# Whole 8 KB rows for the gate-up matrix of the experts, with gate and up summed at the same time in two banks

## What is computed

```python
def moe_ffn(x, w_router, b_router, w_gu, b_gu, w_down, b_down):
    ...
    def expert_block(args):
        xb, e = args
        h = xb @ w_gu[e] + b_gu[e]              # w_gu[e] is 1024 x 2048
        h_gate, h_up = jnp.split(h, 2, axis=-1)
        h_gate = jnp.minimum(h_gate, SWIGLU_LIMIT)
        h_up = jnp.clip(h_up, -SWIGLU_LIMIT, SWIGLU_LIMIT)
        act = h_gate * jax.nn.sigmoid(SWIGLU_ALPHA * h_gate) * (h_up + 1.0)
        return act @ w_down[e] + b_down[e]      # w_down[e] is 1024 x 1024
```

## Time and profile before

| | us |
|---|---|
| median of 3 runs | 2260.23 |
| lowest and highest of them | 2252.01, 2263.8 |
| the profiled execution | 2261.8 |
| its span in the profile | 2260.0 |
| TensorE busy in it | 2079.9 |

### The profile page before, as it was taken

One profiled execution on the slowest core, in us unless ns is written; L12 is line 12 of the kernel. 1 busy time (PEld: TensorE's weight loads), 2 busy tenths in 40 slices (PEclk: granted clock), 3 DMA queues, 4 the chain that ended last, 5 costly groups with the idle time before them and its releaser, 6 DMA issues.

```text
span 2260.0 us, 27915 instructions
## 1 busy us (share of the span) xinstructions
PE 2079.9 (92%) x11973; PEld 1381.1 (61%) x11973; DVE 831.3 (37%) x961; ACT 698.4 (31%) x922; POOL 35.0 (2%) x26
## 2 busy tenths in 40 slices
PE   7999989999999997899998999988988988898886
PEld 6998778899899775799977544423333333333222
DVE  5555745555555584555543511111111101111102
ACT  5444454544544534444334211111111111111111
POOL 5000000000000000000000000000000000000000
PEclk9999999999999995999999999999999999999998
DMA  8555416555455440355544799999999999999995
GB/s 277 193 186 184 142 29 205 186 186 182 153 188 185 164 148 22 112 187 186 186 158 144 257 405 412 412 413 413 413 413 413 413 413 412 413 414 413 413 413 236
DMA packets 225239, 604.25 MB, mean 267 GB/s; under 512 B 12276, under 2 KB 105408, under 8 KB 208660
## 3 DMA queue, kind: packets, MB, share of 16 engines
q1 hardware_dynamic: 225140, 602.83, 71.7%
HBM read 601.70 MB, written 1.09 MB: 267 GB/s over the span
## 4 chain that ended last, share of the span: by engine, by line
PE 62%; DMA 28%; DVE 5%; ACT 2%; issue 1%; SPq 1%; ACTq 0%; DVEq 0%
PE ps L1366 14%; PE ps L1367 14%; PE ps L1368 14%; DMA sb_w_free<-in_moe_w_gate_up 12%; PE ps L1684 12%; DMA sb_raw<-in_moe_w_gate_up 7%; DMA sb_late_raw<-in_moe_w_gate_up 6%; PE ps L1667 2%; PE ps L1539 1%; PE ps L1500 1%; DMA sb_more_raw<-in_moe_w_gate_up 1%; DMA sb_raw<-in_moe_w_down 1%; PE ps L1524 1%; PE ps L1509 1%; PE ps L1386 1%
## 5 line engine op out<-in xcount | busy, mean ns | idle before, releaser
L843 DVE TENSOR_TENSOR sb_w_lo<-sb_raw,sb_w_hi 128x2048 fp32r<-128x2048 f32 x180 | 416.2, 2316 | 358.8 <-ACT sb_w_hi L582 358.4
L582 ACT ACTIVATE sb_w_hi<-sb_raw 128x2048 fp32r<-128x2048 f32 x180 | 343.9, 1914 | 295.1 <-PE ps L1368 282.8
L1366 PE MATMUL ps<-sb_xT_hi,sb_w_hi 128*128 128x256 f32 x1408 | 397.3, 282 | 7.4 <-DVE sb_xT_lo L864 7.4
L1367 PE MATMUL ps<-sb_xT_lo,sb_w_hi 128*128 128x256 f32 x1408 | 396.2, 281 | 0.0
L1368 PE MATMUL ps<-sb_xT_hi,sb_w_lo 128*128 128x256 f32 x1408 | 396.1, 281 | 0.0
L1366 PEld LDWEIGHTS ps<-sb_xT_hi,sb_w_hi 128*128 128x128 f32 x1408 | 265.9, 189 | 9.9 <-issue 4.5
L1367 PEld LDWEIGHTS ps<-sb_xT_lo,sb_w_hi 128*128 128x128 f32 x1408 | 266.0, 189 | 1.6
L1368 PEld LDWEIGHTS ps<-sb_xT_hi,sb_w_lo 128*128 128x128 f32 x1408 | 266.0, 189 | 0.0
L1684 PE MATMUL ps<-sb_raw,sb_xs 128*64 128x512 f32 x792 | 190.8, 605 | 22.8 <-DMA sb_raw<-in_moe_w_gate_up 22.8
L1684 PE MATMUL ps<-sb_w_free,sb_xs 128*64 128x512 f32 x736 | 176.8, 604 | 21.0 <-DMA sb_w_free<-in_moe_w_gate_up 20.9
L770 ACT ACTIVATE sb_x<-ps 128x512 f32<-128x512 f32 x64 | 38.2, 597 | 492.2 <-PE ps L1684 492.2
(11 more groups left out here) (236 smaller groups left out, 2340.4 us busy)
## 6 DMA issues: line engine op xcount, KB each, us to landing
sb_raw<-in_moe_w_gate_up SPq DMA_DIRECT2D x99, 1024.0 KB, 20.8
sb_w_free<-in_moe_w_gate_up SPq DMA_DIRECT2D x92, 1024.0 KB, 20.9
sb_w_free<-in_moe_w_down SPq DMA_DIRECT2D x52, 1024.0 KB, 19.4
sb_raw<-in_moe_w_down SPq DMA_DIRECT2D x45, 1024.0 KB, 18.3
sb_raw<-in_ffn_w_gate SPq DMA_DIRECT2D x44, 1024.0 KB, 5.3
sb_raw<-in_ffn_w_up SPq DMA_DIRECT2D x44, 1024.0 KB, 5.3
sb_raw<-in_ffn_w_down SPq DMA_DIRECT2D x44, 1024.0 KB, 4.9
sb_late_raw<-in_moe_w_gate_up SPq DMA_DIRECT2D x32, 1024.0 KB, 19.1
```

What stands on the lines that cost most here:

```text
L582: sc.activation(w_hi[:, c % CUT, :], raw[:, c % RAW, :], ACT.Copy).then_inc(hi_made, 1)
L843: ve.tensor_tensor(w_lo[:, c % CUT, :], raw[:, c % RAW, :], w_hi[:, c % CUT, :].bitcast(F32), ALU.subtract).then_inc(lo_made, 1)
L1366: pe.matmul(o, l_hi, r_hi, start=start, stop=False)
L1367: pe.matmul(o, l_hi, r_lo, start=False, stop=False)
```

## The change

Three things change together.

- **Loads.** The gate-up matrix of an expert is loaded in 8 chunks of 128 whole rows, 8 KB a row, one row in each partition. The down chunks stay. The order in step s is 3 gate-up chunks of the next expert, 4 down chunks of this one, 5 gate-up chunks of the next, again 12 chunks a step and 384 in all, in the same ring.
- **Sums.** A gate-up chunk feeds both sums at once, two matmuls into bank 0 (gate) and two into bank 1 (up), all four with the same 64 tokens' 128 rows as weights. Bank 2 takes down, bank 3 the picks, gathered rows and gate turned.
- **Reading.** After the last gate-up chunk ScalarE copies bank 0 and VectorE copies bank 1 to the two halves of h_rows (now 1024 wide), and TensorE turns both, gate into bank 3 and up into bank 2, at the start of the next step. The scatter now stands behind the last gate-up chunk, where it stood ahead of the last up chunk.

```diff
@@ expert_chunk, step_loads (SyncE)
-                w = a["moe_w_down_2"][0] if part == "down" else a["moe_w_gate_up_2"][0]
-                col = D if part == "up" else 0
-                rows = "e (p k) n -> p (e k) n" if part == "down" else "e (k p) n -> p (e k) n"
-                src = w[bass.ds(e, 1), 256 * j:256 * (j + 1), col:col + D].rearrange(rows, p=P)
+                if part == "down":
+                    src = a["moe_w_down_2"][0][bass.ds(e, 1), 256 * j:256 * (j + 1), :].rearrange("e (p k) n -> p (e k) n", p=P)
+                else:
+                    src = a["moe_w_gate_up_2"][0][bass.ds(e, 1), P * j:P * (j + 1), :].rearrange("e p n -> p e n")
...
+                for j in range(first, 3):
+                    expert_chunk("gate_up", e + 1, j, step_t(s) + j, laps)
                 for j in range(4):
...
+                    if 3 + j >= first:
+                        expert_chunk("down", e, j, step_t(s) + 3 + j, laps)
+                for j in range(3, 8):
+                    if 4 + j >= first:
+                        expert_chunk("gate_up", e + 1, j, step_t(s) + 4 + j, laps)
@@ ScalarE and VectorE
+            def read_gate(t, laps):
+
                 sc.wait_ge(chunk_used, used_no(t, laps))
...
+                sc.activation(h_rows[:, 0, :], ps[:, 0, :], ACT.Copy).then_inc(gate_read, 1)
...
+            def read_up(t, laps):
+
+                ve.wait_ge(chunk_used, used_no(t, laps))
+                ve.tensor_copy(h_rows[:, 1, :], ps[:, 1, :]).then_inc(up_read, 1)
@@ TensorE
+            def gate_up_rows(left, t, i, laps):
+
+                pe.wait_ge(slot_loaded[t % RING], loaded_no(t, laps))
+                for bank in range(2):
+                    for h in range(2):
+                        w = slots[t % RING][:, bank * D + h * 512:bank * D + (h + 1) * 512]
+                        ins = pe.matmul(ps[halves[h], bank, :], left(i), w, start=False, stop=i == KT - 1)
+                ins.then_inc(chunk_used, 1)
...
             def first_step(r):
...
                 bias(0, 0, 0)
+                bias(1, D, 0)
                 for j in range(4):
                     pe.wait_ge(xs_made, n + j + 1)
-                    rows(left, j, j, 0, laps)
+                    gate_up_rows(left, 2 * j, 2 * j, laps)
                     if j < 2:
                         gather(2 + j, 0, 2 + j)
...
+                    gate_up_rows(left, 2 * j + 1, 2 * j + 1, laps)
+                    if j < 2 and isinstance(r, int):
+                        residual(1, j)
...
             def step(base, base4, s, laps):
...
+                pe.wait_ge(gate_read, e + 1)
+                turn_rows(0, 3)
+                pe.wait_ge(up_read, e + 1)
+                turn_rows(1, 2)
...
+                bias(0, 0, s + 1)
+                bias(1, D, s + 1)
+                for i in range(3):
+                    gate_up_rows(left, t + i, i, laps)
+                pe.wait_ge(m_g_made, e + 1)
+                turn_picks(base4, s)
                 pe.wait_ge(m_act_made, e + 1)
...
+                for j in range(4):
+                    down_rows(t + 3 + j, j, laps)
...
+                for i in range(3, 8):
+                    gate_up_rows(left, t + 4 + i, i, laps)
                 pe.wait_ge(y_lo_made, e + 1)
                 scatter()
-                rows(left, t + 11, 3, q, laps)
```

More of the change, by code:

```diff
@@ L463, in _ @@
[L463 to L470, removed]
+                dst = slots[t % RING].rearrange("p (a n) -> p a n", a=2 if part == "down" else 1)
+                sp.dma_start(dst, src).then_inc(slot_loaded[t % RING], 16)
@@ L503, in more_loads @@
                 laps = round_laps(r)
[L504 to L507, removed]
+                for j in range(8):
+                    expert_chunk("gate_up", 0, j, j, laps)
                 with sp.Fori(0, N_E // 4 - 1) as it:
@@ L1683, in rows, with turn_rows @@
                         w = slots[t % RING][:, k * D + h * 512:k * D + (h + 1) * 512]
-                        ins = pe.matmul(ps[halves[h], bank, :], left(2 * j + k), w,
-                                        start=not biased and j == 0 and k == 0, stop=j == 3 and k == 1)
+                        ins = pe.matmul(ps[halves[h], 2, :], own(2 * j + k), w, start=j == 0 and k == 0, stop=j == 3 and k == 1)
                 ins.then_inc(chunk_used, 1)
-            def turn_rows(n, bank):
-                pe.wait_ge(h_read, n)
-                by_row = h_rows.rearrange("q (j p k) -> q j k p", j=2, k=2)
+            def turn_rows(part, bank):
+                by_row = h_rows[:, part, :].rearrange("q (j p k) -> q j k p", j=2, k=2)
                 for i in range(4):
@@ L1701, in turn_picks @@
                     for half in halves:
-                        pe.matmul(ps[half, bank, b * P:(b + 1) * P], own, ident[:], start=True, stop=True)
+                        pe.matmul(ps[half, 3, b * P:(b + 1) * P], own, ident[:], start=True, stop=True)
                 for half in halves:
@@ L1705, in turn_picks @@
                         own = pick[:, (s // 4) % 2, b, SLOTS * (s % 4):SLOTS * (s % 4 + 1)].bitcast(F32)
[L1706 removed]
+                        ins = pe.matmul(ps[half, 3, S:S + 1], own, quad_gate[:, (s // 4) % 2, b, s % 4:s % 4 + 1],
                                         start=b == 0, stop=b == 1)
@@ L1760, in step @@
-                for j in range(1, 4):
-                    rows(own, t + 4 + j, j, p, laps)
-                pe.wait_ge(m_g_made, e + 2)
-                if s < PIECES:
-                    pe.wait_ge(xs_made, e + 6)
-                bias(q, D, s + 1)
-                for j in range(3):
-                    rows(left, t + 8 + j, j, q, laps)
+                    pe.wait_ge(pickT_made, e + 1)
+                    gather(3, (s + 5) // 4, (s + 5) % 4)
+                for i in range(3, 8):
+                    gate_up_rows(left, t + 4 + i, i, laps)
@@ L1788, in last_step @@
                     ins.then_inc(down_bias_added, 1)
+                pe.wait_ge(m_g_made, e + 1)
+                turn_picks(QUADS * r, s)
                 pe.wait_ge(m_act_made, e + 1)
-                pe.wait_ge(pickT_made, e + 1)
                 for j in range(4):
-                    rows(own, t + j, j, 0, laps, biased=False)
+                    down_rows(t + j, j, laps)
                 pe.wait_ge(y_lo_made, e + 1)
```

163 lines of the change are left out of this document (67 added, 96 removed).

## The result

The changed kernel takes 2246.53 us (median of 20 runs, 2240.66 to 2263.64), the kernel before 2261.11 (20 runs, 2252.01 to 2275.73). The ratio is 0.9937, 95% interval 0.9918 to 0.9956, or 14.6 us less where 25.9 were forecast. The profiled executions are 17.2 us apart, 2260.0 and 2242.8 us of span.

The account below looks back on a forecast made before the run. DMA transfers were taken to bound the expert stage. From 2260.23 us, loads 26.7 less, start 0, TensorE 0 and end 0.8 more, 25.9 less in all, gave 2234.3 us; range 2223 to 2250.

Parts of the forecast that it names:

- What bounds it: Mixture-of-experts stage: DMA transfers set the pace from about 1500 us, 30.41 us a step; TensorE needs 25.65.
- Loads, 26.7 us: Expert stage: gate-up chunks in 8 KB rows land every 2.46 us, 0.89 us less a step, over 30 steps.
- the choice between 2.46 and 2.49 us: Landing interval of 8 KB-row chunks: 2.46 from the last three down chunks, taken, or 2.49 from all four.
- rival A: Expert-stage loads: long rows land every 2.49 us, step 29.88, gain 15.9 us, kernel 2245.1 us; chance 0.18.
- The rule on packets: Expert-stage loads: some 3 cycles overhead a packet, by estimate a step 0.24 us shorter, kernel 7 us, 2254.
- The start, 0: Beginning of the expert stage: first slots are freed for a steady stream equally early, 0, with 1 us either side.
- TensorE in the steady state, 0: Expert steps: TensorE's step stays near 25.65 us, 3.9 below the new 29.52, so no time changes.
- The end, +0.8: Behind the last gate-up chunk: chain to down 8.9 us instead of 7.6, 1.3 longer, 0.5 given back.

Follow-up runs that it names:

- e1: Changed kernel with gate-up chunks fetched as in the kernel before, two 4 KB pieces for each partition; ratio to before 1.0015.
- e2: Kernel before with down chunks also in two 4 KB pieces for each partition, so all pieces are short; ratio to before 1.0055.
- e3: Changed kernel with gate-up chunks of whole 8 KB rows lying 64 KB apart instead of one contiguous megabyte; ratio to before 0.9926.
- e6: Changed kernel with down chunks in two 4 KB pieces for each partition; ratio to before 0.9993.
- e4: Changed kernel with gate-up chunks in four 2 KB pieces for each partition; one run, 2312.45 us.
- e8: Kernel before with TensorE's waits for m_act_made and pickT_made one chunk earlier; one run, 921.6 us from first to last output copy (before 921.0).
- e7: Changed kernel without VectorE's branch and loop for further rounds, which these inputs never enter, ahead of the last norm; one run, 2248.64 us.

## Why the forecast was right in kind and its gain too large

**What bounds it.** Right. The stretch is paced by the landing of chunks before and after, and TensorE's spare time never entered: e1 with the new order and the old pieces takes the old time.

**Loads, 26.7 us.** This is the term that was wrong: 30 x 0.59, 17.7 us, came of it. The last gate-up chunk lands 18.0 us earlier in all. The cause, rows of 8 KB instead of 4 KB, is shown by e1, e2, e3, e6 and e4. The failed step is the choice between 2.46 and 2.49 us: I took three intervals of four because three agreed. They agreed because the first of the four started late, for a reason of TensorE's own (e8), so that they had 0.1 us less to span. So the start of a waiting matmul is the landing of its chunk only where it has nothing else to wait for. The four together, 9.96 us or 2.49 each, held the answer, and rival A priced it: 2245.1, against 2246.53 measured. That a step in seven or eight is 1.2 to 1.5 us late stayed in after (31.33, 31.20); what makes it late no run shows.

The remark of "HBM Reference" in the Trainium skill, about 425 GB/s for a core alone, seemed to support 426; it stands in the section "Specifications (TRN2)", not in "Access". The steady rate is 421 by the windows.

**The rule on packets**, from the Trainium skill's "DMA: Bandwidth & Descriptors", section "Why small descriptors are slow (HBM only)", would by my estimate have given 7 us and 2254. 17.7 us were measured, and 9 ns a packet; this kernel's packets cost more than the rule's three cycles, which is what the rows had said, at a somewhat smaller size.

**The start, 0.** About right: of the 18.0 us by which the last gate-up chunk lands earlier, the steps explain 17.7. The first copy of after stands 1.3 us earlier (1323.75 against 1325.07), although the stage began 0.8 us later in that execution.

**TensorE in the steady state, 0.** Right: 25.45 us for an early step, clock 1.00.

**The end, +0.8.** The chain to the first down matmul was less long than forecast (7.7, not 8.9) and the down chunks ran in 8.63 instead of 9.50, both within the bounds given for the clock. Against it stand 1.9 us for VectorE's jump, which I didn't see. The forecast counted instructions of TensorE and none of the code that is only jumped over. From the last gate-up chunk's landing to the end of the span it is 33.5 us in before and 34.2 in after: 0.8 more, the very number forecast, but by luck: chain and down chunks together came out 2.1 us shorter than forecast, and the jump, 1.9 us, wasn't in it.

**The sum by the profiles**: the last gate-up chunk 18.0 earlier, 0.8 lost behind it: 17.2. (By the copies: the first 1.3 earlier, 17.8 less from first to last, 0.9 of it by the quicker down chunks at the end, and 1.9 lost behind the last.) The 17.2 lie within the interval of the ratio (9.9 to 18.5 us), whose middle is the 14.6 of the medians; the 25.9 of the forecast don't.

## What to carry to other kernels

Where a stretch is bound by transfers, count packets, not only bytes: at 1 MB a load, going from 4 KB to 8 KB pieces was worth 3% of the load's time here, and from 2 KB to 4 KB 6%. Where the 8 KB pieces lay, side by side or 64 KB apart, made no difference. When you read landings from the starts of the waiting instructions, take a whole period of like chunks; an instruction with more semaphores than its neighbours starts late by itself and makes the next interval look quick. And look at what stands behind the last load: work there that doesn't need it, like the bias products here, can go into any earlier step in which the engine waits.

## What the hardware showed that I had not expected

- A packet costs an engine 9 to 9.5 ns, straight over 8, 16 and 32 packets for an engine and megabyte (2.485, 2.558 and 2.71 us).
- More bytes wait in the queue when the pieces are longer: issue to landing is 14.8 us where most pieces have 2 KB (e4), 20.8 where most have 4 KB (before) and 26.4 with 8 KB (after). Divided by the interval between landings that is an estimated 5 to 6, 8, and 10 to 11 chunks.
- A matmul with two semaphores more to wait for starts about 0.1 us late although they are met (e8, e2).
- From VectorE's branch to the first instruction behind the jump it is 0.6 us in before and 2.9 in after, whose code in between is longer; it cost 1.9 us at the end (e7).
- The scatter of the runs (2252 to 2276 us of before) seems for the larger part made in the first 1300 us: the first output copy stands at 1322 to 1342 us in eleven traces, while the stretch behind it repeats within 0.7 us (903.2, 903.6, 903.8).
